# When the second weight panel's remainder is formed, at seven norm boundaries of a two-block transformer kernel

## The reference

```
h = modulate(rms_norm(x, g_pre), shift, scale)
x = x + gate * rms_norm(f(h), g_post)
```

```
h = h + 0.5 * rmsnorm(swiglu(rmsnorm(h, g_pre_ffn1), w_ffn1_gu, w_ffn1_down), g_post_ffn1)
mix = token_mixer(rmsnorm(h, g_pre_mix), ...)        # attention + gated linear attention + w_out
h = h + rmsnorm(mix, g_post_mix)
h = h + 0.5 * rmsnorm(swiglu(rmsnorm(h, g_pre_ffn2), w_ffn2_gu, w_ffn2_down), g_post_ffn2)
```

## Time and profile before

| | |
|---|---|
| median of 3 timed runs | 2459.97 us (2455.49 to 2460.3) |
| the profiled execution's own time | 2458.33 us |
| its span | 2456.5 us |
| PE busy | 2099.5 us (85%) |
| DVE busy | 1361.2 us (55%) |
| ACT busy | 968.6 us (39%) |
| share of the closing chain | PE 76%, DVE 12%, DVE's queue 4%, ACT 3% |
| mean granted clock of PE | 0.875 |

### The profile page before, as it was taken

One profiled execution on the slowest core, in us unless ns is written; L12 is line 12 of the kernel. 1 busy time (PEld: TensorE's weight loads), 2 busy tenths in 40 slices (PEclk: granted clock), 3 DMA queues, 4 the chain that ended last, 5 costly groups with the idle time before them and its releaser, 6 DMA issues.

```text
span 2456.5 us, 38752 instructions
## 1 busy us (share of the span) xinstructions
PE 2099.5 (85%) x14928; PEld 1981.6 (81%) x14928; DVE 1361.2 (55%) x2067; ACT 968.6 (39%) x1405; POOL 80.7 (3%) x104
## 2 busy tenths in 40 slices
PE   2799656888789989998989589997999898778997
PEld 1699546887679979997976578997999796567997
DVE  3876536444666555555443476655664644356664
ACT  1233234332345435533452245534542344234542
POOL 0240101000000000000000000000000000000000
PEclk9799867777789989999975699998999997578999
DMA  6366000000335534543420043452454341023452
GB/s 261 135 242 256 35 23 1 0 0 17 122 120 182 199 116 165 187 162 112 171 86 1 3 154 137 171 188 100 174 188 146 121 176 63 1 77 129 180 199 100
DMA packets 44373, 300.93 MB, mean 123 GB/s; under 512 B 5712, under 2 KB 7904, under 8 KB 12032
## 3 DMA queue, kind: packets, MB, share of 16 engines
q1 hardware_dynamic: 41648, 295.85, 33.1%
q10 hardware_dynamic: 2224, 2.28, 0.3%
q0 software_dynamic: 416, 1.64, 0.2%
HBM read 298.70 MB, written 1.05 MB: 122 GB/s over the span
## 4 chain that ended last, share of the span: by engine, by line
PE 76%; DVE 12%; DVEq 4%; ACT 3%; issue 3%; DMA 1%; POOLq 0%; POOL 0%; ACTq 0%
PE acc L614 20%; PE acc L616 19%; PE acc L615 19%; DVE w_lo L596 2%; PE acc L1841 2%; PE mb L1813 1%; PE mb L1812 1%; ACT w_hi L589 1%; DVE rstd L751 1%; PE mb L1398 1%; PE mb L810 1%; PE acc L1398 1%; DVEq L960 1%; DMA x<-in_meta 1%; PE mb L1395 1%
## 5 line engine op out<-in xcount | busy, mean ns | idle before, releaser
L614 PE MATMUL acc<-h_hi,w_hi 128*128 128x272 f32 (+1 forms) x3040 | 882.0, 290 | 59.1 <-DVE h_lo L800 28.2
L615 PE MATMUL acc<-h_lo,w_hi 128*128 128x272 f32 (+1 forms) x3040 | 877.3, 289 | 0.0
L616 PE MATMUL acc<-h_hi,w_lo 128*128 128x272 f32 (+1 forms) x3040 | 875.4, 288 | 0.0
L596 DVE TENSOR_TENSOR w_lo<-land,w_hi 128x2048 fp32r<-128x2048 f32 (+2 forms) x257 | 590.4, 2299 | 265.6 <-ACT w_hi L589 265.3
L614 PEld LDWEIGHTS acc<-h_hi,w_hi 128*128 128x128 f32 x3040 | 582.4, 192 | 64.7 <-issue 40.1
L589 ACT ACTIVATE w_hi<-land 128x2048 fp32r<-128x2048 f32 (+2 forms) x257 | 490.8, 1911 | 305.8 <-PE acc L616 270.1
L616 PEld LDWEIGHTS acc<-h_hi,w_lo 128*128 128x128 f32 x3040 | 584.8, 192 | 0.0
L615 PEld LDWEIGHTS acc<-h_lo,w_hi 128*128 128x128 f32 x3040 | 584.4, 192 | 0.1
L614 PE MATMUL acc<-a_hi,w_hi 128*128 128x272 f32 (+1 forms) x880 | 251.4, 286 | 0.8 <-DVE w_lo L596 0.7
L616 PE MATMUL acc<-a_hi,w_lo 128*128 128x272 f32 (+1 forms) x880 | 251.5, 286 | 0.0
L615 PE MATMUL acc<-a_lo,w_hi 128*128 128x272 f32 (+1 forms) x880 | 250.4, 285 | 0.0
(11 more groups left out here) (465 smaller groups left out, 2566.0 us busy)
## 6 DMA issues: line engine op xcount, KB each, us to landing
land<-in_w_gu SPq DMA_DIRECT2D x110, 1024.0 KB, 4.8
land<-in_w_in SPq DMA_DIRECT2D x65, 1024.0 KB, 4.8
land<-in_w_down SPq DMA_DIRECT2D x40, 1408.0 KB, 6.1
ada_first<-in_w_ada SPq DMA_DIRECT2D x24, 1024.0 KB, 4.9
land<-in_w_ab SPq DMA_DIRECT2D x24, 512.0 KB, 3.2
land<-in_w_out SPq DMA_DIRECT2D x12, 1024.0 KB, 4.9
land<-in_w_in_single SPq DMA_DIRECT2D x6, 512.0 KB, 3.2
const<-in_const ACTq DMA_DIRECT2D x1, 1134.0 KB, 40.3
```

The costliest lines, as they stand in the source:

```text
L596: k.nc.vector.tensor_tensor(k.w_lo[:, p.par, 0:size * P], k.land[:, p.par, 0:size * P], k.w_hi[:, p.par, 0:size * P].bitcast(F32), ALU.sub ...
L614: mm(out, k.w_hi[:, par, c], hi, start=start, stop=False)
L615: mm(out, k.w_hi[:, par, c], lo, start=False, stop=False)
L616: return mm(out, k.w_lo[:, par, c], hi, start=False, stop=stop)
```

## The change

`dve_post` loses its `late` split. `dve_pre` gets B as an argument (`second`) and forms B's `w_lo` as its last step, behind the last `h_lo`, at all seven norms. At norms 2 and 5 the prologues go; the down section before them is told the sizes of the next panels, so that ACT splits A and B in `w_hi` behind its last two panels and DVE splits A in `w_lo` behind the last but one, as at the other norms.

```diff
-def dve_pre(k, dve, i, W, gain, shift=None):
+def dve_pre(k, dve, i, W, gain, second, shift=None):
     dve_rstd(k, dve, i * 2, W)
     dve_pre_apply(k, dve, i, W, gain, shift)
+    split_lo(k, dve, Panel.of(second[0], second[2]), second[1])
+    dve.drain()
...
-def dve_post(k, dve, i, W, gain, late=None, loop=0):
+def dve_post(k, dve, i, W, gain):
...
     v.memset(k.ssum[:, :], 0.0)
-    if late is not None:
-        split_lo(k, dve, Panel.of(late[0], loop), late[1])
     dve.drain()
...
 def dve_ffn(k, dve, i, gu, down, post, W, gain, nxt, loop=0):
...
-    late = None if nxt[1] is None else (down + DOWN + 1, nxt[1])
-    dve_post(k, dve, post, W, gain, late, loop)
+    dve_post(k, dve, post, W, gain)
...
 # ScalarE's program
-    act_ffn(k, act, 0, M_GU1, M_DOWN1, 1, W1, (None, None))
+    act_ffn(k, act, 0, M_GU1, M_DOWN1, 1, W1, (GU_K, GU_K))
     for l in range(LAYERS):
...
-        prologue(split_hi, k, act, M_LAYER, GU_K, loop)
+        end = (GU_K, GU_K) if l + 1 < LAYERS else (None, None)
...
-        act_ffn(k, act, l * 2 + 2, M_LAYER + L_GUB, M_LAYER + L_DOWNB, l * 3 + 4, W, (None, None), loop)
+        act_ffn(k, act, l * 2 + 2, M_LAYER + L_GUB, M_LAYER + L_DOWNB, l * 3 + 4, W, end, loop)
...
 # VectorE's program
-    dve_post(k, dve, 0, W1, lambda t: k.fold[:, 1, t:t + 1], (M_GU1 + 1, GU_K))
-    dve_pre(k, dve, 1, W1, lambda t: k.fold[:, 2, t:t + 1], lambda t: k.mod[:, 24 + t:25 + t])
-    dve_ffn(k, dve, 0, M_GU1, M_DOWN1, 1, W1, lambda t: k.fold[:, 3, t:t + 1], (None, None))
+    dve_post(k, dve, 0, W1, lambda t: k.fold[:, 1, t:t + 1])
+    dve_pre(k, dve, 1, W1, lambda t: k.fold[:, 2, t:t + 1], (M_GU1 + 1, GU_K, 0), lambda t: k.mod[:, 24 + t:25 + t])
+    dve_ffn(k, dve, 0, M_GU1, M_DOWN1, 1, W1, lambda t: k.fold[:, 3, t:t + 1], (GU_K, GU_K))
     for l in range(LAYERS):
...
-        prologue(split_lo, k, dve, M_LAYER, GU_K, loop)
-        dve_pre(k, dve, l * 3 + 2, W2, gain("pre1"))
+        end = (GU_K, GU_K) if l + 1 < LAYERS else (None, None)
+        dve_pre(k, dve, l * 3 + 2, W2, gain("pre1"), (M_LAYER + L_GUA + 1, GU_K, loop))
...
-        dve_pre(k, dve, l * 3 + 3, W2, gain("pre_mix"))
+        dve_pre(k, dve, l * 3 + 3, W2, gain("pre_mix"), (M_LAYER + L_SINGLE + 1, AB_K, loop))
...
-        dve_post(k, dve, l * 3 + 3, W, gain("post_mix"), (M_LAYER + L_GUB + 1, GU_K), loop)
-        dve_pre(k, dve, l * 3 + 4, W, gain("pre2"))
+        dve_post(k, dve, l * 3 + 3, W, gain("post_mix"))
+        dve_pre(k, dve, l * 3 + 4, W, gain("pre2"), (M_LAYER + L_GUB + 1, GU_K, loop))
         dve_ffn(k, dve, l * 2 + 2, M_LAYER + L_GUB, M_LAYER + L_DOWNB, l * 3 + 4, W, gain("post2"),
-                (None, None), loop)
+                end, loop)
```

## The result

The changed kernel took 2465.3 us (median of 8, 2459.16 to 2467.05) against 2455.76 us for the kernel before, timed again beside it (median of 8, 2454.44 to 2460.3). The ratio is 1.0036 with a 95% interval of 1.0026 to 1.0046, some 9 us. The profiled execution after has a span of 2460.8 us, 4.3 more than before, at a mean granted clock of 0.873 (before 0.875). It had gained 2.7 us before norm 1, where nothing was changed; counted from norm 1's first reciprocal, the change cost 6.9 us in it.

A forecast was written before the change was run, and what follows sets the result against it. PE's large products set the pace, so the change acts only at the hinges where PE waits. Gains of 2.8 us and losses of 7.9 gave +5.1 on 2458.33, or 2463.4 us, range 2457.5 to 2468.5.

The forecast's parts named there:

- The late load of D: Norms 3 and 6: D's load, released later by B's remainder, delays D by 2.4 us each, 4.8 us lost.
- the rivals: For this figure, norms 3 and 6: D's load is hidden if it takes under 2.6 us; 2456.9 us, chance 0.13.
- The clock behind the gap: Before D at norms 3 and 6: PE's longer idle time lowers its clock, 1.55 us lost each, 3.1 together.
- Norms 2 and 5: Second reciprocal comes sooner without prologues, despite a later first root: gains of 0.9 and 1.2 us.
- The page's price of a table switch: First root at norms 2 and 5: a switch costs about 2.66 us, adding 2.1 to the forecast; chance 0.03.
- Norms 1 and 4: Second reciprocal no longer waits for B's remainder, which stays hidden under panel A: gains of 0.5 and 0.2 us.
- The sum: All norms: 2.8 us gained and 7.9 lost, together +5.1 us, giving 2463.4 us.

The follow-up runs named there:

- pair of half loads: Kernel before with B's remainder behind h_lo at norms 3 and 6, D's load halved: released late 2462.23 us (1.0033), released early 2457.98 us (1.0018).
- norms 3 and 6 alone: Kernel before with B's remainder moved behind h_lo only at norms 3 and 6: 2468.02 us, ratio 1.0044; repeated, 2467.3 us, 1.0043.
- the old place: Kernel with splits ahead at norms 2 and 5 and B's w_hi behind the first root, but B's remainder in dve_post at all norms: 2447.66 us, 0.9963.

## Why the prediction was right, step by step

It forecast 2463.4 us in 2457.5 to 2468.5, and slower as the likeliest by a little; measured were 2465.3. Part of this nearness is luck. The forecast stands on a base of 2458.33 us, and the kernel before took 2455.76 when timed beside the changed one. The change itself was forecast at +5.1 us and measured +8.8 (6.4 to 11.3): the direction and the mechanism were right, the size was too small.

**The late load of D** (2 x 2.4 us). Right in mechanism and size. Its three numbers were met: 4.92 us from B's remainder to ACT's split of D (4.99), idle time before D 2.96 and 3.09 us (3.2), D later by 2.25 us behind norm 3's reciprocal and by 2.38 behind norm 6's. The pair of half loads shows the cause. B itself began 0.66 us later behind the reciprocal (9.73 less 9.07; 0.7 predicted), 0.5 us of it idle time of PE. One figure of the rivals is wrong: from 1137.45 to 1140.75 it is 3.3 us, not the 2.6 from which the load would have been hidden. Its 4.92 us were too long for either.

**The clock behind the gap** (2 x 1.55). Right in mechanism, too small in size: both gaps were followed by the lower clock, at a price of 6 x 0.49 = 2.9 and 6 x 0.28 = 1.7 us in the changed profile, 4.6 instead of 3.1. The same 4.6 stands in both profiles of norms 3 and 6 alone (0.72 and 0.51 each). All six gaps of 2.96 to 3.09 us before D were followed by a clock of 0.51 or 0.72. The three waits of the earlier trace rows were a weak base for them. In all 14 kept profiles w_out's three waits, 2.6 to 3.0 us but for one of 4.16, are followed by a clock below 1 over the next 6 us in 28 of 42 cases: always in the first block, 5 times in layer 0, 9 times in layer 1. The mean loss over these 42 is about 1.6 us, which is what was predicted; D's gaps cost 2.3 on average.

**Norms 2 and 5** (−0.9, −1.2). Norm 2 gained 0.36 and norm 5 1.52: 1.9 together against 2.1. The sum was met, but each norm missed by 0.3 to 0.5 us, in opposite directions. The delay of the root was as computed: 3.50 us from square to root at norm 2. The page's price of a table switch (the Trainium skill, "ScalarE: Activation LUTs", "What ACT_TABLE_LOAD costs", 2.66 us) did not appear: the load took 1.28 us and the root began 0.02 us behind it. What I passed over is that this delay could be avoided by exchanging two steps. The root would then come 1.4 us earlier at norm 2, and the version that does it is the only one here that is clearly faster than the kernel before.

**Norms 1 and 4** (−0.5, −0.2). The reciprocals gained 0.50 and 0.61. But at norm 1 PE waited 0.21 us for B, which I had called hidden. At norms 2, 4, 5 and 7 it did not wait. So the moved remainder has no cover to spare at norm 1, and there the comparison with the old place shows no gain left.

**The sum.** −2.8 and +7.9 gave +5.1. In the changed profile, counted from norm 1, the mixers hold +11.7 and the rest −4.8, together +6.9; the timing says +8.8 (6.4 to 11.3). The term that was sized too small is the loss in the mixers: 11.7 against 7.9. The rest gained 4.8 where 2.8 was forecast, which hid half of that miss; no run isolates these 2 us.

D's lateness (2.25 + 2.38) and the windows behind it (4.6) explain 9.2 of the 11.7. The other 2.5 us lie later in the mixers, where nothing was changed. More than half of it is at w_out's wait in layer 1, which was followed by a clock of 1.00 before and by 0.74 now, 6 x 0.26 = 1.6 us:

```profile
2210.94:2216.94 6.00, 6.00 (x39) 6.00 (x40) 4.22 (x6) 1.11 (x2) 0.00 (x0) 0.74 0.63 203
```

This is not only the one profile. In the three profiles with the late load, w_out's waits in the two layers were followed by a clock below 1 in 6 of 6 cases; in the seven with norms 3 and 6 as before, in 3 of 14. That D's lateness is what brings this about is likely by these counts, but no run isolates it, and the remaining 0.9 us of the 2.5 stays open. The mean granted clock over the two mixers went from 0.79 and 0.81 to 0.78 and 0.79:

```profile
1124.23:1468.87 344.64, 290.97 (x1770) 260.07 (x1770) 164.89 (x287) 126.72 (x233) 5.27 (x7) 0.78 0.26 92
1917.03:2239.14 322.11, 271.99 (x1714) 241.69 (x1714) 158.84 (x256) 121.85 (x209) 4.74 (x6) 0.79 0.28 98
```

## What to carry to other kernels

A split or copy that frees a landing buffer also issues the next load. Before moving it to where the engine is idle, follow what it releases: here 1.2 us of work, moved behind a short panel, made a load start 11 us later (from 0.7 us before the second reciprocal to 9.9 behind it), and at two places that cost some 11 us. The distance to watch is from the release to the next use of the buffer, against release-to-use of a load that did wait (4.9 us here); one panel of 3 us behind the release didn't cover it, one of 6 us at the other norms did.

And when a chain of small steps crosses engines, look at the order inside each of them first. Putting one copy (1.1 to 1.9 us) behind a root instead of ahead of it at four hinges, together with splitting ahead, took 7 to 8 us off, 2.5 of which may be the clock's scatter. Moving the remainder made no difference there that could be told.

## What the runs showed of the hardware that was not expected

An idle time of PE of 3 us inside a stretch where it is otherwise busy can be followed by the lower clock, and its length alone doesn't say whether it is. Of the 48 such gaps in the 14 profiles (42 before w_out's panels, 6 before the late D) 34 were followed by a clock below 1 and 14 were not, with lengths of 2.6 to 3.0 us on both sides. Of shorter ones before D, one of 1.93 us was followed by 0.72, one of 1.78 us by 1.00, and all 16 of 1.47 us by 1.00. The matmul stream that bridged the gap kept the clock at 1.00 in 4 of 4 cases.

A kernel of one core also scatters with this: the kernel before ran between 2446.19 and 2460.57 us over 35 runs beside the second set, with mean granted clocks from 0.874 to 0.881, and its fastest runs are among those with the highest clock. A ratio then has an interval of 0.1 to 0.15% each way, which is why the single gains of 1 to 3 us here stay undecided.
